# Gate projections moved beside the gated recurrence, experts in 32-row column tiles, and queries padded with zeros

## The chip, the cores and the metric

One core of one Trainium2 chip runs the whole program. The metric is the device time of one execution in microseconds (us). TensorE (PE) multiplies, VectorE (DVE) and ScalarE (ACT) work on rows, GpSimd (POOL) issues the scatters, SyncE (SP) issues the loads and stores.

## The reference

Everything is float32. `first_block` adds to x (512 tokens of 1024) the sum of an attention branch and a recurrent branch, each through a gate projected from the same normed rows h:

```python
o_b = rms_norm(o_fwd + o_bwd, hg_norm_w[layer]) * jax.nn.silu(g_b.reshape(B, S, HG_HEADS, HG_DV))
y_b = jnp.einsum('bsc,cd->bsd', o_b.reshape(B, S, HG_WIDTH), w_proj_b[layer].astype(f32))
merged = jax.nn.sigmoid(zgate_a) * y_a + jax.nn.sigmoid(zgate_b) * y_b
h_res = h_res + jnp.einsum('bsd,de->bse', merged, w_out[layer].astype(f32))
```

Then two layers work on x and, in the first of them, on 256 context rows as well. Layer 0 mixes with a dense attention and a convolution, layer 1 with a recurrence and an attention over a neighbourhood (8 heads of 64, 512 queries, local keys and 256 context keys). Each ends with 16 experts that choose their tokens: 64 of x, and in layer 0 also 32 of the context, each through w1, w3 and w2 of 1024x1024:

```python
hid = jax.nn.silu(jnp.einsum('becd,edf->becf', xs, w1)) * jnp.einsum('becd,edf->becf', xs, w3)
ys = jnp.einsum('becf,efd->becd', hid, w2) * gate[..., None].astype(h.dtype)
```

## The kernel before

The program is written by hand, engine by engine, with semaphores. Every float32 matmul is two instructions in the trace, so an "x4" in an order of instructions is "x8" in the trace.

**First block.** `first_block` (L1179) runs the attention (`first_attention`, L619), then the gated recurrence (L1023) and the modulation (L1249) turn by turn: `weave` takes one turn of each generator in rotation, with six PSUM banks for the recurrence and two for the other line. The modulation has 48 turns, each one load of 1 MB (two slots, L1284) and four matmuls (L1308), two columns each, at the four column tiles. The recurrence goes through blocks of heads: a head of the block with large products (L1069, L1081, L1098, L1118), then a loop over chunks (update L1128, read-out L1152, both directions). The tail stands behind it (L1199 to L1241): Square of recurrentT (L1204), sums by ones (L1205), L1207, Sqrt (L1210), one reciprocal of 128x4096 (L1212), two multiplications, the g_b projection with Silu (`dense` at L373, activation L1218), a multiplication (L1221), proj_b (L377), the two other gates with Sigmoid (L1231), L1234 and L1236, 32 transposes, w_out, whose results are added to the rows at L1239. `dense` loads weights 2 MB at a time in a ring; L373 is its form with the weights stationary and the tokens moving, L377 that with the tokens stationary. `core.settle(engine)` lets an engine wait until everything loaded and computed so far is there.

**Experts of layer 0.** `experts` (L1501) has a ring of six slots of 2 MB, each half of the columns of a weight, in rows of 512 columns (L1550). Per expert, 128 matmuls hold a 128x128 tile of weights and move the 96 tokens (L1574), and 16 hold 96 columns of hidden values and move 512 columns of w2 (L1588). Silu is at L1604, the product at L1617, two scatters per expert add to `row_sums` and `context_sums`. Layer 1 has 64 tokens per expert and does it otherwise: `experts_in_tiles` (L1668) holds 64 columns of tokens in each of two column tiles and moves the weights (L1737).

**Neighbourhood.** `neighbourhood` (L2618) gives 32 units (8 heads x 4 tiles of 128 queries) to `attend` (L1953): scores (L1989, keys and queries on 64 rows, two heads in the halves of 128 partitions), transposes (L2041), weights times values (L2069). The dense attention of layer 0 uses the same `attend` with 96 rows.

## Time and profile before

| | us |
|---|---|
| runs timed | 5477.23, 5398.36, 5399.64 |
| their median | 5399.64 |
| profiled execution, its own time | 5478.97 |
| its span | 5477.2 |
| mean granted clock of TensorE | 0.824 of full speed |

| stage | from | to |
|---|---|---|
| recurrence beside modulation | about 796 | 1284 |
| tail of the first block | 1284 | 1619 |
| experts of layer 0 | 2564 | 3290 |
| units of the neighbourhood | about 4547 | 4730 |
| experts of layer 1 | about 4920 | 5477 |

The stages stand one behind the other, so a stage that gets shorter by some us brings its whole gain to the end unless the next one waits for something else. In the rows below "start us, us" are the start and the busy time of a run of like instructions, "xN" is their count, and the bracket at the end gives the idle time before them and what ended it. PEclk is the granted clock: 1.00 is full speed (2.4 GHz), 0.50 the half (1.2 GHz).

### The profile page before, as it was taken

To read this page: it belongs to the slowest core of one execution; us is meant where nothing else is said; L and a number is where in the kernel's file an instruction comes from. 1 tells how busy PE (TensorE), PEld (TensorE's weight loads), DVE (VectorE), ACT (ScalarE), POOL (GpSimd) and SP (SyncE) were. 2 spreads that over 40 slices of the span, in tenths; PEclk is the share of its full clock that TensorE was granted. 3 is DMA by queue.
4 is the path that set the end of the run, shared out by engine and by line. 5 is a ranking of instruction groups with operands and counts; after the bars stand their busy time and mean duration, and the time that the engine had idled before them with its cause. 6 is when DMAs were issued, how large, how long until landed. Compare 5 with 4: busy or idle time off the path is not lost. (4 is left out here: it accounts for less than half of the span.)

```text
span 5477.2 us, 55057 instructions
## 1 busy us (share of the span) xinstructions
PE 4162.9 (76%) x23087; PEld 2861.7 (52%) x23087; DVE 1573.8 (29%) x2699; ACT 649.2 (12%) x1292; POOL 88.1 (2%) x72
## 2 busy tenths in 40 slices
PE   7987879897978245863999996658788579837777
PEld 4674467663434124733777773357677437622222
DVE  2222223234011746522111112354554422230000
ACT  1121010101010012300000000022212101110000
POOL 0000000000000000000000000000000000000000
PEclk9987995767989667986999997877888786668898
DMA  3100223232201000113888861100000010129999
GB/s 115 62 1 31 88 77 108 93 108 98 102 31 52 0 21 1 38 49 130 310 302 300 306 221 62 46 10 2 1 2 2 26 55 12 44 81 383 382 382 340
DMA packets 317051, 612.86 MB, mean 112 GB/s; under 512 B 32380, under 2 KB 68460, under 8 KB 310150
## 3 DMA queue, kind: packets, MB, share of 16 engines
q1 hardware_dynamic: 309574, 588.35, 30.1%
q0 software_dynamic: 7232, 20.98, 1.6%
q8 instruction: 186, 3.05, 0.2%
q14 instruction: 59, 0.48, 0.0%
HBM read 582.94 MB, written 26.36 MB: 111 GB/s over the span
## 5 line engine op out<-in xcount | busy, mean ns | idle before, releaser
L377 PE MATMUL bank<-weights_l,hT_l 128*128 128x512 f32 (+3 forms) x2080 | 714.3, 506 | 56.2 <-DMA weights_l<-in_od_w_in 21.2
L377 PEld LDWEIGHTS bank<-weights_l,hT_l 128*128 128x128 f32 (+1 forms) x2080 | 435.6, 213 | 331.9 <-issue 265.8
L1574 PE MATMUL bank<-expert_tokensT_l,expert_weights_l 128*128 128x96 f32 x4096 | 462.8, 276 | 23.0 <-DMA expert_weights_l<-in_moe_w 23.0
L1574 PEld LDWEIGHTS bank<-expert_tokensT_l,expert_weights_l 128*128 128x128 f32 x4096 | 463.0, 193 | 30.8 <-issue 30.8
L373 PE MATMUL bank<-hT_l,weights_l 128*128 128x512 f32 (+1 forms) x1056 | 384.4, 527 | 46.6 <-DMA weights_l<-in_w_in 23.9
L1737 PE MATMUL bank<-expert_weights_l,expert_tokensT_l 128*64 128x512 f32 x1024 | 258.7, 663 | 113.4 <-DMA expert_weights_l<-in_moe_w 113.4
L373 PEld LDWEIGHTS bank<-hT_l,weights_l 128*128 128x128 f32 x1056 | 203.6, 193 | 226.2 <-issue 184.6
L1737 PEld LDWEIGHTS bank<-expert_weights_l,expert_tokensT_l 128*64 128x64 f32 x1024 | 91.1, 152 | 270.7 <-issue 270.7
L1588 PE MATMUL bank<-expert_weights_l,hidden_l 128*96 128x512 f32 x512 | 223.6, 594 | 10.1 <-DVE hidden_l L1617 10.1
L1737 PE MATMUL bank<-expert_weights_l,hiddenT_l 128*64 128x512 f32 x512 | 129.3, 663 | 45.3 <-DMA expert_weights_l<-in_moe_w 45.3
L377 PE MATMUL bank<-weights_l,mixedT_l 128*128 128x512 f32 x320 | 141.7, 606 | 29.1 <-DMA weights_l<-in_od_w_out 15.0
L1588 PEld LDWEIGHTS bank<-expert_weights_l,hidden_l 128*96 128x96 f32 x512 | 82.2, 163 | 140.4 <-issue 127.7
L1617 DVE TENSOR_TENSOR hidden_l<-silu_l,bank 128x96 f32<-128x96 f32 x128 | 32.6, 255 | 427.6 <-ACT silu_l L1604 427.6
L2041 PE MATMUL bank<-identity,scores_l 128*128 128x128 f32 (+1 forms) x704 | 131.0, 340 | 7.7 <-ACT scores_l L2027 7.7
L2041 PEld LDWEIGHTS bank<-identity,scores_l 128*128 128x128 f32 (+1 forms) x704 | 112.8, 236 | 40.0 <-issue 26.6
L377 PE MATMUL bank<-weights_l,recurrentT_l 128*128 128x512 f32 x256 | 112.4, 601 | 19.4 <-DMA weights_l<-in_w_proj_b 18.4
L1989 PE MATMUL bank<-kT_l,qT_l 64*128 64x256 f32 (+3 forms) x288 | 120.4, 550 | 1.5 <-DVE kT_l L313 1.5
L377 PEld LDWEIGHTS bank<-weights_l,mixedT_l 128*128 128x128 f32 x320 | 62.2, 195 | 107.5 <-issue 107.5
L1896 DVE SCALAR_TENSOR_TENSOR convolved_l<-padded_l,taps_l,convolved_l 128x798 f32<-128x798 f32 x120 | 117.9, 1046 | 1.1
L1128 PEld LDWEIGHTS bank<-values_l,rows 32*128 32x128 f32 x480 | 94.0, 292 | 44.5 <-DVE state_l L1143 33.7
L1800 DVE TENSOR_TENSOR hidden_l<-silu_l,bank 128x512 f32<-128x512 f32 x16 | 11.0, 688 | 362.0 <-PE bank L1737 362.0
L1152 PEld LDWEIGHTS bank<-queries_scaled_l,state_l 128*128 128x128 f32 x480 | 103.8, 320 | 20.5 <-issue 12.0
(435 smaller groups left out, 5095.9 us busy)
## 6 DMA issues: line engine op xcount, KB each, us to landing
expert_weights_l<-in_moe_w SPq DMA_DIRECT2D x192, 2048.0 KB, 18.6
ada_weights_r<-in_ada_w SPq DMA_DIRECT2D x48, 1024.0 KB, 4.9
weights_l<-in_w_in SPq DMA_DIRECT2D x16, 2048.0 KB, 7.9
weights_l<-in_w_in SPq DMA_DIRECT2D x16, 1024.0 KB, 5.1
weights_l<-in_od_w_in SPq DMA_DIRECT2D x7, 1024.0 KB, 5.3
weights_l<-in_ev_w_in SPq DMA_DIRECT2D x3, 2048.0 KB, 10.5
weights_l<-in_od_w_in SPq DMA_DIRECT2D x3, 2048.0 KB, 7.8
weights_l<-in_w_proj_b SPq DMA_DIRECT2D x2, 2048.0 KB, 15.0
```

The lines of the kernel that those rows point to most:

```text
L373: ins = pe.matmul(bank[:n, :m], w_sb[:, k, s:s + n], xT[:, k, t:t + m], start=k == 0, stop=k == kt - 1)
L377: ins = pe.matmul(bank[:rows_of_tile(x), :n], x, w_sb[:, k, :n], start=k == 0, stop=k == kt - 1)
L1128: ins = pe.matmul(kv_bank[i % 2][:, hh * P:hh * P + P], ks[r, c // 4, hh * P:hh * P + P], v[r, c // 4, hc + hh * P:hc + hh * P + P], start ...
L1152: ins = pe.matmul(o_bank[hh][:, c * CH:c * CH + CH], state[:, i % 2, hh * P:hh * P + P], qt[:, hh, c * CH:c * CH + CH], start=False, stop= ...
L1574: ins = pe.matmul(bank[:, m * 256:m * 256 + S], w[:, k, (f % 4) * P:(f % 4) * P + P], xs[:, k, e, 0:S], start=k == 0, stop=k == KT - 1)
L1588: ins = pe.matmul(core.bank[3 + h][:S, :], hid[:, e % 2, f, :], w[:, f, :], start=f == 0, stop=f == KT - 1)
L1617: dve.tensor_tensor(hid[:, e % 2, f, :], act_out[:, g % 3, :], core.bank[g % 3][:, 256:256 + S], ALU.mult).then_inc(hid_done.sem, hid_done ...
L1737: ins = pe.matmul(bank[h * S:h * S + S, :], rows(k), ring[2 * (i % PAIRS) + h][:, k, :], start=k == 0, stop=k == KT - 1)
L1800: dve.tensor_tensor(hid[:, e % 2, :], silu[:, e % 2, :], core.bank[2 + e % 2][:, :], ALU.mult) \
L1896: ins = dve.scalar_tensor_tensor(out=conv[:, c, :], in0=h[:, c, k:k + OUT], scalar=taps[:, c, k:k + 1], in1=conv[:, c, :], op0=ALU.mult, o ...
L1989: ins = pe.matmul(s_bank[n % 2 * 2 + j][:, a:b], q, k, start=True, stop=True)
L2041: ins = pe.matmul(t_bank[m % 2][:b - a, i * P:i * P + P], s[:, n % R, a:b], core.ident[:, :], start=True, stop=True)
```

## The change

`gate_products` is a third generator in `weave`: 48 turns of four matmuls for the g_b, z_b and z_a projections of the first block (weights stationary, tokens moving), with 12 loads of 1 MB into one slot, a copy by ACT and a store of 256 KB to DRAM for every 128 columns. The modulation goes from two slots to one and from two banks to one; the gates have the other. Both branches are kept by columns (proj_a and proj_b transposed). The tail loads the three gates, the attention branch (2 MB each) and the context rows from DRAM, prefetches w_proj_b, and works in halves; `take` multiplies and adds as the banks of proj_b come, and the transposes are gone. `experts_in_strips` stands for `experts`: four column tiles of 32 tokens, weights moving, eight slots of 2 MB with rows of 1024 columns, hidden values turned by `turn`, three scatters per expert into one tensor of sums (the third waits for the second). The buffers lie in X. In the neighbourhood qT gets a plane per head, whose other half is zero, and the keys go in with all 128 rows.

```diff
+        merge_groups(core, I, C, flip, lasting, hT, top, den, u,
+                     ya[:, :, :].rearrange("p t (a n) -> p (t a) n", n=SEQ))
...
-              lambda e, tt, col, n, ps: copy(core, e, ya[:, tt, col:col + n], ps), ready=False)
+              lambda e, ct, t0, n, ps: copy(core, e, ya[:, ct, t0:t0 + n], ps), transposed=True, ready=False)
...
+def gate_products(core, I, hT, w, out, kept):
...
+    landed, copied = core.weights[1], core.emptied_s
...
+    W, DEEP = 2 * P, KT // 2
...
+    chunks = [(j, off, c) for j, off in enumerate((OFF_GB, OFF_ZGB, OFF_ZGA)) for c in range(0, D, W)]
...
+    for j, off, c in chunks:
+        if n:
+            sp.wait_ge(summed.sem, n)
+        weight_load(w[:, :, :], I["w_in"], KT, off + c, W)(sp).then_inc(landed.sem, landed.sixteen())
+        for s in range(0, W, P):
+            for half in range(2):
+                yield True
+                if half == 0:
+                    pe.wait_ge(landed.sem, landed.n)
+                    if n:
+                        pe.wait_ge(copied.sem, at + n)
+                for k in range(half * DEEP, half * DEEP + DEEP):
+                    ins = pe.matmul(bank[:, :], w[:, k, s:s + P], hT[:, k, :], start=k == 0, stop=k == KT - 1)
+            ins.then_inc(summed.sem, summed.one())
+            n += 1
+            act.wait_ge(summed.sem, n)
+            if n > 1:
+                act.wait_ge(stored.sem, 16 * (n - 1))
+            act.copy(out[:, :], bank[:, :]).then_inc(copied.sem, copied.one())
+            sp.wait_ge(copied.sem, at + n)
+            sp.dma_start(kept[j][:, (c + s) // P, :], out[:, :]).then_inc(stored.sem, stored.sixteen())
+    sp.wait_ge(stored.sem, stored.n)
...
-            core.store(spill, ya[:, :, :])
+            core.store(spill, ya[:, :, :].rearrange("p t (a n) -> p (t a) n", n=SEQ))
...
-            with core.beside(6) as other:
+            with core.beside(6) as other, other.scope() as beside:
+                w, rows = beside("gate_weights", [P, KT, 2 * P]), beside("gate_rows", [P, SEQ])
                 weave(gated_recurrence(core, I, C, hT, oT, X[:, NT:NX, :].rearrange("p t (a b) -> p (t a) b", b=HB * P)),
-                      modulation(other, I, C, mod_dram))
-            core.load(X[:, NT:NX, :], I["ctx_2"][0].rearrange("(t p) d -> p t d", p=P))
+                      gate_products(other, I, hT, w, rows, gates), modulation(other, I, C, mod_dram))
...
+                early = prefetch(core, HH, I["w_proj_b"], 0, D)
...
+                    ya, yb, za, zb = (sb3(name, [P, KT, SEQ]) for name in (
+                        "attention_outT", "recurrence_outT", "attention_gateT", "recurrence_gateT"))
...
+                    gates_landed = [Signal(nc, f"gate_landed_{j}") for j in range(3)]
+                    for dst, src, signal in zip((gb, zb, za), gates, gates_landed):
+                        sp.dma_start(dst[:, :, :], src).then_inc(signal.sem, signal.sixteen())
+                    core.load(ya[:, :, :], spill)
+                    core.load(X[:, NT:NX, :], I["ctx_2"][0].rearrange("(t p) d -> p t d", p=P))
+                    half = HH // 2
...
                     core.settle(act)
-                    act.activation(sq[:, :, :], oT[:, :, :], ACT.Square).then_inc(step.sem, step.one())
+                    for a in range(0, HH, half):
+                        act.activation(sq[:, a:a + half, :], oT[:, a:a + half, :], ACT.Square).then_inc(step.sem, step.one())
...
-                    act.activation(gb[:, :, :], gb[:, :, :], ACT.Sqrt).then_inc(step.sem, step.one())
+                    for a in range(0, HH, half):
+                        act.wait_ge(core.emptied_v.sem, core.emptied_v.n - HH + a + half)
+                        act.activation(rstd[:, a:a + half, :], rstd[:, a:a + half, :], ACT.Sqrt) \
+                            .then_inc(rooted.sem, rooted.one())
+                    act.wait_ge(gates_landed[0].sem, 16)
+                    act.activation(gb[:, :, :], gb[:, :, :], ACT.Silu).then_inc(step.sem, step.one())
+                    gated = step.n
...
+                        s = slice(a, a + half)
+                        dve.wait_ge(rooted.sem, i + 1)
+                        linked(dve, core.link_v, dve.reciprocal(rstd[:, s, :], rstd[:, s, :]))
+                        linked(dve, core.link_v, dve.tensor_tensor(oT[:, s, :], oT[:, s, :], rstd[:, s, :], ALU.mult))
+                    dve.wait_ge(step.sem, gated)
+                    dve.wait_ge(landed.sem, landed.n)
+                    for a in range(0, HH, half):
+                        dve.scalar_tensor_tensor(out=oT[:, a:a + half, :], in0=oT[:, a:a + half, :], scalar=w[:, 0:1],
+                                                 in1=gb[:, a:a + half, :], op0=ALU.mult, op1=ALU.mult) \
+                            .then_inc(step.sem, step.one())
+                    for gate, signal in ((zb, gates_landed[1]), (za, gates_landed[2])):
+                        act.wait_ge(signal.sem, 16)
+                        act.activation(gate[:, :, :], gate[:, :, :], ACT.Sigmoid).then_inc(step.sem, step.one())
                     dve.wait_ge(step.sem, step.n)
-                    dve.reciprocal(gb[:, :, :], gb[:, :, :]).then_inc(step.sem, step.one())
-                    dve.wait_ge(step.sem, step.n)
...
-                    dense(core, hT, KT, SEQ, I["w_in"], OFF_GB, D,
-                          lambda e, ct, t0, n, ps: e.activation(gb[:, ct, t0:t0 + n], ps, ACT.Silu),
-                          transposed=True, who=lambda i: "s")
-                    core.settle(dve)
...
-                with core.scope() as sb3:
...
-                    core.load(ya[:, :, :], spill)
-                    dense(core, oT, HH, SEQ, I["w_proj_b"], 0, D,
...
-                        dense(core, hT, KT, SEQ, I["w_in"], off, D,
...
-                        dve.tensor_tensor(y[:, :, :], y[:, :, :], g[:, :, :], ALU.mult).then_inc(step.sem, step.one())
...
-                    transpose_tokens(core, ya, oT, NT, C["ident"])
-                dense(core, oT, KT, SEQ, I["w_out"], 0, D,
...
+                    dve.tensor_tensor(ya[:, :, :], ya[:, :, :], za[:, :, :], ALU.mult).then_inc(step.sem, step.one())
+                    def take(e, ct, t0, n, ps):
+                        linked(e, core.link_v, e.tensor_tensor(yb[:, ct, t0:t0 + n], ps, zb[:, ct, t0:t0 + n], ALU.mult))
+                        return e.tensor_tensor(yb[:, ct, t0:t0 + n], yb[:, ct, t0:t0 + n], ya[:, ct, t0:t0 + n], ALU.add)
+                    dense(core, oT, HH, SEQ, I["w_proj_b"], 0, D, take, transposed=True, who=lambda i: "v", ready=False,
+                          early=early)
+                    dense(core, yb, KT, SEQ, I["w_out"], 0, D,
+                          lambda e, tt, col, n, ps: e.tensor_tensor(X[:, tt, col:col + n], X[:, tt, col:col + n],
+                                                                    ps, ALU.add), who=lambda i: "v", ready=False)
...
-        slot = [sb("ada_weights", [P, DEEP, W]) for _ in range(2)]
-        mod = sb("bias_then_mod", [P, 2, BANK])
...
-            sp.dma_start(slot[i % 2][:, :, :],
...
+            if i:
+                sp.wait_ge(used.sem, i)
+            sp.dma_start(slot[:, :], dram(I["ada_w_2"][block // per], k * P * MOD + block % per * W, [[MOD, P], [1, W]])) \
...
-def experts(core, I, C, X, layer, nx, mod_dram, sel_dram, xs, sums):
+def experts_in_strips(core, I, C, X, layer, mod_dram, sel_dram, xs, sums):
...
+    STRIP = P // 4
...
+    SLOTS = 8
...
-                    eng_ins = sp.dma_start(ring[n % RING][:, :, :], dram(src, h * HALF, [[D, P], [P * D, KT], [1, HALF]]))
...
+                for i, (name, e, half) in enumerate(plan):
+                    if i >= SLOTS:
+                        sp.wait_ge(used.sem, free_at[i - SLOTS])
+                    sp.dma_start(ring[i % SLOTS][:, :, :], dram(I[name][layer, e], half * DEEP * P * D,
+                                                                [[D, P], [P * D, DEEP], [1, D]])) \
...
-                            for k in range(KT):
-                                ins = pe.matmul(bank[:, m * 256:m * 256 + S], w[:, k, (f % 4) * P:(f % 4) * P + P],
-                                                xs[:, k, e, 0:S], start=k == 0, stop=k == KT - 1)
...
-                            ins = pe.matmul(core.bank[3 + h][:S, :], hid[:, e % 2, f, :], w[:, f, :],
-                                            start=f == 0, stop=f == KT - 1)
...
+                def hidden(e, half):
+                    if half == 0 and e:
...
+                    w1, w3 = landed("moe_w1_2", e, half), landed("moe_w3_2", e, half)
+                    for j in range(DEEP):
+                        k = half * DEEP + j
...
+                        def strip(bank, q, w, h, g):
+                            return pe.matmul(bank[q * STRIP:(q + 1) * STRIP, :], xs[:, k, e, g * STRIP:(g + 1) * STRIP],
+                                             w[:, j, h * HALF:(h + 1) * HALF], start=k == 0, stop=k == KT - 1)
+                        for q, (h, g) in enumerate(pairs[:4]):
+                            strip(w1_bank, q, w1, h, g)
+                        for q, (h, g) in enumerate(pairs[:4]):
+                            strip(w3_bank, q, w3, h, g)
+                        for q, (w, (h, g)) in enumerate(((w1, pairs[4]), (w1, pairs[5]), (w3, pairs[4]), (w3, pairs[5]))):
+                            ins = strip(rest_bank, q, w, h, g)
+                    ins.then_inc(used.sem, used.one())
...
+                    for c in range(4):
+                        pe.transpose(turn_bank[:, c * P:c * P + P], hid[:, c * P:c * P + P], C["ident"][:, :])
+                    for c in range(4):
+                        ins = pe.matmul(turn_bank_b[:, c * 2 * STRIP:(c + 1) * 2 * STRIP], hid_b[2 * STRIP:, c * P:c * P + P],
+                                        C["ident"][2 * STRIP:, 2 * STRIP:], start=True, stop=True)
...
+                    for f in range(half * DEEP, half * DEEP + DEEP, 2):
+                        for j in range(2):
+                            for q, (m, g) in enumerate(pairs[:4]):
+                                strip(y_bank, q, f + j, m, g, 0, KT - 1)
+                        for j in range(2):
+                            for q, (m, g) in enumerate(pairs[4:]):
+                                ins = strip(y_bank_b, 2 * j + q, f + j, m, g, j, KT - 2 + j)
...
+                hidden(0, 0)
+                hidden(0, 1)
                 for e in range(NE):
-                    hidden(e)
-                    output(e)
+                    if e + 1 < NE:
+                        hidden(e + 1, 0)
+                    turn(e)
+                    if e + 1 < NE:
+                        hidden(e + 1, 1)
+                    output(e, 0)
...
+                    for i, (j, at) in enumerate(((0, slice(0, P)), (1, slice(0, 2 * STRIP)), (1, slice(2 * STRIP, P)))):
+                        if i == 2:
+                            pool.wait_ge(scattered[1].sem, 16 * (e + 1))
                         pool.indirect_dma_start(
-                            out=sums[1], out_offset=bass.IndirectOffsetOnAxis(ap=idx[0:CAP_C, 1, e:e + 1], axis=0),
-                            in_=ysc[:, e % 2, :], in_offset=None, compute_op=ALU.add) \
...
+                            out=half_rows, out_offset=bass.IndirectOffsetOnAxis(ap=idx[0:at.stop - at.start, j, e:e + 1], axis=0),
+                            in_=ys[j][at, :], in_offset=None, compute_op=ALU.add) \
...
         v = sb("v_and_one", [P, len(V0) + NC, NA_H, NA_D + 1])
-        qT = sb("qT", [P, NA_H // 2, SEQ])
...
+        for c in range(NA_H // 2):
+            dve.memset(qT[NA_D:, 2 * c, :], 0.0).then_inc(step.sem, step.one())
+            dve.memset(qT[:NA_D, 2 * c + 1, :], 0.0).then_inc(step.sem, step.one())
...
-                transpose_tokens(core, x[0], qT, NT, C["ident"])
...
+                def take(e, c, bank):
+                    copy(core, e, qT[:NA_D, 2 * c, :], bank[:NA_D, :])
+                    return copy(core, e, qT[NA_D:, 2 * c + 1, :], bank[NA_D:, :])
+                products(core, NA_H // 2, fill, take, turns)
...
-                r = slice(h % 2 * NA_D, h % 2 * NA_D + NA_D)
...
-                    q = qT[r, h // 2, t * P:t * P + P]
+                    q = qT[:, h, t * P:t * P + P]
...
-                    parts = [((at, LOCAL + CTX), [(at, LOCAL, q, kTt[r, h // 2, a:b]),
...
+                    parts = [((at, LOCAL + CTX), [(at, LOCAL, q, kTt[:, h // 2, a:b]),
```

On TensorE, in the loop of the recurrence, one round before is:

```order
L1128 MATMUL bank<-values_l,rows 128x128 x4
L1152 MATMUL bank<-queries_scaled_l,state_l 128x32 x4
L1128 MATMUL bank<-values_l,rows 128x128 x4
L1152 MATMUL bank<-queries_scaled_l,state_l 128x32 x4
L1308 MATMUL bank<-ada_weights_r,conditionsT_r 2x512 x4
```

and one round after it:

```order
L1131 MATMUL bank<-values_l,rows 128x128 x4
L1155 MATMUL bank<-queries_scaled_l,state_l 128x32 x4
L1131 MATMUL bank<-values_l,rows 128x128 x4
L1155 MATMUL bank<-queries_scaled_l,state_l 128x32 x4
L1209 MATMUL bank<-hT_l,gate_weights_r 128x512 x4
L1357 MATMUL bank<-ada_weights_r,conditionsT_r 2x512 x4
```

Each round has four matmuls more, ahead of the modulation's. On SP, at the start of the tail, before:

```order
L140 DMA rows<-in_ctx 128x2x1024
L140 DMA gain_l<-in_hg_norm_w 128x1
L323 DMA weights_l<-in_w_in 128x8x512 x2
L140 DMA attention_out_l<-rows_spilled 128x4096
L323 DMA weights_l<-in_w_proj_b 128x8x512 x2
```

and after:

```order
L323 DMA weights_l<-in_w_proj_b 128x8x512 x2
L140 DMA gain_l<-in_hg_norm_w 128x1
L1250 DMA gateT_l<-gate 128x4096
L1250 DMA recurrence_gateT_l<-gate 128x4096
L1250 DMA attention_gateT_l<-gate 128x4096
L140 DMA attention_outT_l<-attention_outT 128x4096
L140 DMA rows<-in_ctx 128x2x1024
```

The context rows, for which ACT waits ahead of Square, now stand last of seven. On TensorE, in the experts of layer 0, one expert before:

```order
L1574 MATMUL bank<-expert_tokensT_l,expert_weights_l 128x96 x128
L1588 MATMUL bank<-expert_weights_l,hidden_l 96x512 x16
```

and after:

```order
L1643 MATMUL bank<-expert_weights_l,expert_tokensT_l 32x512 x48
L1659 MATMUL bank<-identity,rows 128x128 x4
L1661 MATMUL bank<-identity,rows 128x64 x4
L1643 MATMUL bank<-expert_weights_l,expert_tokensT_l 32x512 x48
L1678 MATMUL bank<-expert_weights_l,rows 32x512 x48
```

The turn of one expert stands between the halves of the next one's hidden products.

## Rows read from the trace of the kernel before

**Rows 1.** Page, the span in 40 slices: granted clock and GB/s.

```profile
PEclk9987995767989667986999997877888786668898
GB/s 115 62 1 31 88 77 108 93 108 98 102 31 52 0 21 1 38 49 130 310 302 300 306 221 62 46 10 2 1 2 2 26 55 12 44 81 383 382 382 340
```

**Rows 2.** Windows of five stretches: length, then busy us of each engine.

```profile
core 0: us, PE busy (x) PEld busy (x) DVE busy (x) ACT busy (x) POOL busy (x), PEclk, DMA share, GB/s
829.50:887.00 57.50, 57.23 (x245) 43.39 (x248) 16.23 (x52) 0.00 (x0) 0.00 (x0) 0.50 0.33 111
...
4547.00:4730.00 183.00, 181.01 (x618) 143.53 (x619) 56.39 (x184) 33.05 (x62) 0.00 (x0) 0.50 0.04 13
2158.00:2315.00 157.00, 148.38 (x1058) 129.20 (x1056) 95.56 (x261) 52.39 (x119) 0.00 (x0) 1.00 0.02 8
2600.00:3280.00 680.00, 668.92 (x4505) 530.12 (x4503) 78.89 (x189) 31.38 (x125) 41.24 (x30) 1.00 0.82 290
4950.00:5460.00 510.00, 375.73 (x1515) 135.50 (x1511) 21.52 (x30) 17.59 (x30) 21.70 (x14) 0.90 1.05 382
```

**Rows 3.** Timeline of TensorE, two places in the loop of the recurrence.

```profile
838.95 1.89 PE L1308 MATMUL bank<-ada_weights_r,conditionsT_r 128*2 128x512 f32 x8
840.77 2.07 PE L1128 MATMUL bank<-values_l,rows 32*128 32x128 f32 x8
842.77 1.92 PE L1152 MATMUL bank<-queries_scaled_l,state_l 128*128 128x32 f32 x8
...
848.46 1.89 PE L1308 MATMUL bank<-ada_weights_r,conditionsT_r 128*2 128x512 f32 x8
...
1203.72 1.08 PE L1152 MATMUL bank<-queries_scaled_l,state_l 128*128 128x32 f32 x8
1204.73 1.04 PE L1308 MATMUL bank<-ada_weights_r,conditionsT_r 128*2 128x512 f32 x8
1205.70 1.15 PE L1128 MATMUL bank<-values_l,rows 32*128 32x128 f32 x8
```

**Rows 4.** Timeline of the first block's tail.

```profile
1284.47 0.40 SPq L140 DMA_DIRECT2D rows<-in_ctx  x1
...
1292.02 3.62 ACT L1204 ACTIVATE squares_l<-recurrentT_l 128x4096 f32<-128x4096 f32 x1 [105.22 <-DMA gain_l<-in_hg_norm_w]
...
1296.31 9.67 PE L1205 MATMUL bank<-squares_l,ones 128*128 128x512 f32 x16 [16.94 <-ACT squares_l L1204]
...
1311.82 25.75 DVE L1212 RECIPROCAL gateT_l<-gateT_l 128x4096 f32<-128x4096 f32 x1 [5.12 <-ACT gateT_l L1210]
...
1361.67 4.43 DVE L1221 TENSOR_TENSOR recurrentT_l<-recurrentT_l,gateT_l 128x4096 f32<-128x4096 f32 x1 [17.25 <-ACT gateT_l L1218]
...
1379.27 57.21 PE L377 MATMUL bank<-weights_l,recurrentT_l 128*128 128x512 f32 x128 [18.37 <-DMA weights_l<-in_w_proj_b]
...
1618.30 0.69 DVE L1239 TENSOR_TENSOR rows<-rows,bank 128x512 f32<-128x512 f32 x1 [6.18 <-PE bank L377]
```

**Rows 5.** Timeline of both layers' experts.

```profile
2584.97 32.00 PE L1574 MATMUL bank<-expert_tokensT_l,expert_weights_l 128*128 128x96 f32 x256 [23.01 <-DMA expert_weights_l<-in_moe_w]
...
2703.93 13.97 PE L1588 MATMUL bank<-expert_weights_l,hidden_l 128*96 128x512 f32 x32 [0.63 <-DVE hidden_l L1617]
2717.74 28.72 PE L1574 MATMUL bank<-expert_tokensT_l,expert_weights_l 128*128 128x96 f32 x256
...
3289.21 0.37 SPq L140 DMA_DIRECT2D rows<-row_sums  x1
...
4946.36 7.09 PE L1737 MATMUL bank<-expert_weights_l,expert_tokensT_l 128*64 128x512 f32 x32 [1.51 <-DMA expert_weights_l<-in_moe_w]
```

**Rows 6.** Timeline of TensorE, one unit of the neighbourhood, and two rows of layer 0's attention.

```profile
4598.30 2.07 PE L1989 MATMUL bank<-kT_l,qT_l 64*128 64x256 f32 x4
4600.30 2.07 PE L2041 MATMUL bank<-identity,scores_l 128*128 128x128 f32 x8
4602.30 2.16 PE L2069 MATMUL bank<-v_and_one_l,weightsT_l 64*128 64x65 f32 x8
...
2200.64 1.50 PE L2041 MATMUL bank<-identity,scores_l 128*128 128x128 f32 x12
2201.98 1.45 PE L2069 MATMUL bank<-kv_and_one_l,weightsT_l 128*128 128x65 f32 x12
```

353 lines of the change are left out of this document (178 added, 175 removed).

## The prediction

> **What bounds the kernel now.** I read the page's slices first [rows 1]. TensorE's granted clock is between 0.5 and 0.9 in most slices and the DMA is far from full except in the last four, which carry 382 GB/s; so nearly everywhere TensorE is the limit, and the question of each stage is how much it has to do and at which clock. Then the windows of the four stretches that the change touches [rows 2]. In the loop of the recurrence TensorE is busy 57.23 of 57.50 us at clock 0.50. In the neighbourhood it is busy 181.01 of 183 us at 0.50. In the experts of layer 0 it is busy 668.92 of 680 us at 1.00, with the DMA at 290 GB/s. In those of layer 1, with column tiles, it is busy only 375.73 of 510 us and the DMA moves 382 GB/s: there the loads are the limit. Last the timelines of the loop [rows 3], of the tail [rows 4], of the experts [rows 5] and of a unit of the neighbourhood [rows 6].
>
> Durations come from the profiled execution, 5478.97 us (its span 5477.2). It lies 79 us above the median of the runs, 5399.64, and the two other runs lie close together at 5398 to 5400. About 80 us is what one long stage at 0.50 instead of 1.00 costs (the neighbourhood, 183 us, would give back up to 92). The sum is made against 5478.97.
>
> **Experts of layer 0: -140 us.** One period before is 43.2 us, from 2703.93 to the 2747 at which the 13.97 + 28.72 end and the next w2 begins [rows 5]. After it, an expert is 144 matmuls of 32 columns for 128 rows of weights, in groups of four tiles: 24 groups for w1 and w3, 12 for w2, two instructions each per tile. What a group costs in a stream is not in this trace. Bounds: two tiles side by side do 32 instructions of 512 in 7.09 us, 0.44 us per pair [rows 5]; four tiles side by side would do 8 instructions in 0.87 if each tile's two instructions run after each other and the tiles together; the modulation's four tiles alone do 8 in 1.04 with their fill [rows 3]; and if only two tiles could run together it is 4 x 0.44 = 1.76. I take 0.87, the row of the stream. 36 x 0.87 = 31.3, and the turn, 8 small matmuls, about 1.7: 33.0 us. The DMA needs 12.58 MB / 382 GB/s = 32.9 us [rows 2]. Both limits nearly meet, so I take 33.4 a period, 16 x (43.2 - 33.4) = 157 less. Given back: 16 more small loads of gates, numbers and gain at 0.4 to 0.6 us each on SP ahead of the weights, 9 us; at the end the third scatter waits for the second and both must land before the rows are read; the last w2 ends near 3278, the rows are read at 3289.21 [rows 5], 11 us for one landing, and one more is about 8. Together -140. Hidden: Silu and the products by DVE, since a whole expert's period lies between them.
>
> **Tail: -127 us.** Before it lasts from 1284.47 to 1619.0 [rows 4], 334 us: proj_b starts at +94.8, then 57.2 of proj_b, two more gates of the same size, multiplications, transposes and w_out. After it, 2 x 2 MB of w_proj_b, 3 x 2 MB of gates, 2 MB of the branch and 1 MB of context are issued, 13.6 MB, and ACT's settle ahead of Square waits for the last of them: 13.6 / 382 GB/s = 35.7, with the first packet 36.5, where it waited 7.6 before. Queued behind Square are the ones products, Sqrt and the reciprocals, thus all of the chain. Then 3.6 Square, 0.7 to TensorE, 10.4 ones and L1207, 3 Sqrt (with its table), 25.8 for the two half reciprocals, 2 x 2.2 for the multiplications, 5 for the scalar multiplication with Silu(g_b), 4.4 for ya times za: proj_b at +93, so the wait eats what the g_b projection leaves (that was hidden by the reciprocal anyway). Then 57.2 of proj_b, 1.8 for the last take, 56 for w_out: 207. The two gates (2 x 57), the transposes and the additions between leave the path: 334 - 207 = 127. If the loads run at 300 GB/s instead, 10 less.
>
> A rule of the Trainium skill speaks against the first two terms: "DMA: Bandwidth & Descriptors", section Bandwidth, has the HBM side binding at about 358 GB/s per core. By that figure a period would be 35.1 us and the sum about 29 us less. This trace moves 382 GB/s over 510 us [rows 2], and the measurement decides.
>
> **Recurrence beside modulation and gates: +92 us.** The 48 turns of the gates are the work that left the tail. Each is 8 instructions of 128x512. At full clock that is 3.45 us (0.43 x 8, from 57.21 / 128 = 0.447 [rows 4]), at half clock 6.9. About 28 of them stand in full rounds of the loop. A round before is 848.46 - 838.95 = 9.5 us at clock 0.50 [rows 3], and 5.2 us by the rows at full clock (1.97 from 1203.72 to 1205.70, twice the 2.07 of an update and a read-out, 1.0). With the gates it is 8.6 at full clock and 16.4 at half. Why is the loop at 0.50? Its matmuls are on 32 rows or move 32 columns, and where such work fills TensorE the trace grants 0.50 [rows 2, 3]; in the tail and the experts, with 128x512 or 128x96 on full rows, it grants 1.00. With gates both kinds stand in each round, and no row of before has such a mix. Neither end is excluded: the bounds of a round are 8.6 and 16.4. I take 11.2, one third of the way from full clock, as each round then has dense work of the kind that the rows have at 1.00. 32 rounds x 1.7 = 54. Four heads of blocks take three turns each, beside products where TensorE idles some us (+5 each, 20), and the last four turns with nothing to fill, 14. Loads of the one slot: 1 MB lands in some 5 us after the last matmul that used it, inside a round of 11; ends of blocks cost 4. Together 92. The ends: -0.9 x 32 + 39 = +10 (the same other terms at full clock throughout), and 6.9 x 32 + 83 = +304 (the 16 other turns at half clock, 5.2 each).
>
> **Neighbourhood: -70 us.** A unit before is 2.07 + 2.07 + 2.16 = 6.1 us of TensorE, by the window 183 / 32 = 5.7 each, at 0.50 [rows 2, 6]. The scores are then on 128 rows, the rest is unchanged. The same `attend` on 96 rows ran 157 us at 1.00 [rows 2], where eight transposes cost 1.0 (1.50 for 12) and eight products with values 0.97 [rows 6]. So the zeros add no time to an instruction (512 columns move as before) and a unit at full clock is 3.1: 32 x 2.7 = 86 less. Back come 8 us until the clock rises and 6 for eight memsets and eight copies in place of four on DVE and ACT. -72, taken as -70. From the other side: no rise, +6.
>
> **Sum.** -140 - 127 + 92 - 70 = -245: 5479 - 245 = **5234 us**, 3.1% under the median. If the two other runs of before already had the neighbourhood at full clock, that is why they lie at 5399; the changed kernel would then be steadier.
>
> **Rivals.**
> - The recurrence runs at full clock with the gates in it: +10 instead of +92, 5234 - 82 = 5152. For: the tail's dense work has 1.00. Against: 32 of a round's 48 instructions stay small. 0.10.
> - The clock of the neighbourhood stays at 0.50: -70 becomes +6, 5309. For: only a third of a unit's matmuls is changed. Against: layer 0's attention has the same two other thirds. 0.08.
> - A group of four tiles exposes its fill each time, as in the lone group of the modulation: 36 x 1.04 + 1.7 = 39.1 a period, 16 x 5.7 = +91: 5325. 0.08. By the Trainium skill, "TensorE: Matmul & The Clock Gate", Part 3 (packing), three column tiles run 2.38 times as fast as one after another, not three times; the estimate from that is 1.09 us per group and about 5354 us. No run here shows it yet.
> - Slower than before: the loop stays at 0.50 with the gates. Each round then takes 9.5 + 6.9 = 16.4 us and the stage +304 instead of +92: 5234 + 212 = 5446, 0.9% over the median. Its place is the loop's rounds, and it decides from about 14.9 us per round: 32 x 3.7 = 118 more than forecast, and with the other turns' 45 the sum reaches the median. For: all of the loop's first 57 us are at 0.50, at 99% busy. Against: dense products stand in every round. 0.08.
> - Four tiles run only two at a time: 36 x 1.76 + 1.7 = 65 us per expert, 16 x 31.6 = +506: 5740. Against: the modulation's group of 1.04 for 8. 0.04.
>
> **How the numbers follow.** The forecast has 0.62, with its own range 5180 to 5290 from the round (10 to 13 us: 5195 to 5290) and the loads. With the rivals at 0.10, 0.08 and 0.08 on both sides the range is 5150 to 5330; it leaves out the two slower rivals and half of the exposed fill. A measurement of this kernel tells about 2% from no change: faster than 5291.6 has 0.75 (forecast 0.60, full clock 0.10, part of the second rival), within 2% 0.20, over 5507.6 0.05.
>
> **What would show it.** Right: periods of 33 to 34 us in the experts with the DMA near 380 GB/s; the loop's clock between 0.6 and 0.9 and rounds of 10 to 13 us; a wait of some 36 us ahead of Square, ended by the context rows, and a tail of about 207 us; the neighbourhood at 1.00 in about 105 us. Wrong: a group of four at over 1 us in the experts' stream; rounds at 15 us or more; a neighbourhood window at 0.50; or TensorE waiting at the gates for their slot, which would add up to 5 us in each of 12 loads, 60 us.

## The result, and the profile after

The changed kernel takes 5210.96 us (median of 4 runs, 5206.3 to 5212.48) where the kernel before, in 4 runs, takes 5422.14 (5398.36 to 5477.23): ratio 0.9595, 95% interval 0.9512 to 0.9678. Forecast were 5234 us, in a range of 5150 to 5330. The kernel before scatters by 80 us from run to run, the changed one by 6; the experiments on the neighbourhood bear on this. The two profiled executions are compared stage by stage; 5477.2 and 5204.5 us are their spans. Each border but the last, the end of the program, is an instruction that both kernels have (the first product of the recurrence, the first load of the tail, the loads of modulation, selection, sums and spilled rows).

| stage | before | after | change | forecast |
|---|---|---|---|---|
| recurrence beside other lines | 488.3 | 586.2 | +98 | +92 |
| tail of the first block | 334.7 | 205.4 | -129 | -127 |
| layer 0 up to its experts | 901.1 | 898.4 | -3 | 0 |
| experts of layer 0 | 769.0 | 618.9 | -150 | -140 |
| recurrence of layer 1 | 1073.4 | 1073.7 | 0 | 0 |
| neighbourhood and its projections | 458.9 | 370.2 | -89 | -70 |
| experts of layer 1 | 655.7 | 655.3 | 0 | 0 |
| sum | | | -273 | -245 |

The page's slices after, beside [rows 1]: the three slices that lie wholly in the first experts now carry 395 to 396 GB/s, and the slice with most of the neighbourhood's units (4293 to 4423 us) is at 0.9 or more.

```profile
PEclk9988798898788857896699988777888879868998
GB/s 106 64 17 33 77 73 108 145 74 134 196 32 36 19 3 19 1 41 50 232 396 395 395 276 42 57 1 2 2 2 2 3 83 13 63 150 383 381 381 337
```

The windows that answer to [rows 2], in the order loop of the recurrence, experts of layer 0, units of the neighbourhood, experts of layer 1:

```profile
core 0: us, PE busy (x) PEld busy (x) DVE busy (x) ACT busy (x) POOL busy (x), PEclk, DMA share, GB/s
829.50:887.00 57.50, 53.18 (x245) 32.27 (x245) 14.10 (x45) 1.76 (x3) 0.00 (x0) 0.81 0.43 142
...
2600.00:3080.00 480.00, 478.51 (x4400) 157.44 (x4396) 41.82 (x60) 30.70 (x60) 62.77 (x43) 1.00 1.02 389
4370.00:4463.00 93.00, 91.65 (x630) 80.93 (x631) 56.18 (x183) 31.34 (x65) 0.00 (x0) 1.00 0.09 27
4680.00:5190.00 510.00, 371.64 (x1508) 134.20 (x1504) 22.27 (x31) 18.19 (x31) 22.14 (x15) 0.90 1.05 380
```

The loop went from 0.50 to 0.81, the neighbourhood from 0.50 to 1.00. In the experts TensorE is busy in all but 1.5 of 480 us while the DMA share is 1.02: both are full. Layer 1 is as it was.

The timeline of TensorE in one round of the loop, the counterpart of [rows 3]:

```profile
1000.92 1.15 PE L1131 MATMUL bank<-values_l,rows 32*128 32x128 f32 x8
1002.00 1.08 PE L1155 MATMUL bank<-queries_scaled_l,state_l 128*128 128x32 f32 x8
1003.01 1.15 PE L1131 MATMUL bank<-values_l,rows 32*128 32x128 f32 x8
1004.10 1.08 PE L1155 MATMUL bank<-queries_scaled_l,state_l 128*128 128x32 f32 x8
1005.01 5.38 PE L1209 MATMUL bank<-hT_l,gate_weights_r 128*128 128x512 f32 x8
1010.32 1.04 PE L1357 MATMUL bank<-ada_weights_r,conditionsT_r 128*2 128x512 f32 x8
...
1018.57 5.54 PE L1209 MATMUL bank<-hT_l,gate_weights_r 128*128 128x512 f32 x8 [3.03 <-DMA gate_weights_r<-in_w_in]
```

The small products run at full clock now (1.15 and 1.08 where [rows 3] had 2.07 and 1.92), and the gates pay for it: their eight instructions take 5.38 us, not the 3.60 of a turn at full clock (so at 1237.8 us), since the clock drops inside them: over the four small products from 1000 to 1005 us it is 1.00, over the gates' turn from 1005 to 1010.3 it is 0.68. A round is 10.4 us, only 0.9 more than before without any gates. The last row is the exception that recurs: a turn that needs a new load can find it not landed.

The tail, against [rows 4]. The chain runs as forecast, step by step:

```profile
1382.54 1.03 SPq L323 DMA_DIRECT2D weights_l<-in_w_proj_b  x2
...
1389.91 0.51 SPq L140 DMA_DIRECT2D rows<-in_ctx  x1
...
1418.20 3.71 ACT L1257 ACTIVATE squares_l<-recurrentT_l 128x2048 f32<-128x2048 f32 x2 [42.40 <-DMA rows<-in_ctx]
...
1433.40 12.95 DVE L1273 RECIPROCAL recurrence_outT_l<-recurrence_outT_l 128x2048 f32<-128x2048 f32 x1
...
1468.68 4.42 DVE L1285 TENSOR_TENSOR attention_outT_l<-attention_outT_l,attention_gateT_l 128x4096 f32<-128x4096 f32 x1
...
1473.16 7.38 PE L373 MATMUL bank<-recurrentT_l,weights_l 128*128 128x512 f32 x13 [40.52 <-DVE attention_outT_l L1285]
```

Square starts 35.7 us after the first load (36.5 forecast), ended by the context rows, and proj_b 90.6 after it (93 forecast).

An expert of layer 0, against [rows 5]:

```profile
2706.87 10.48 PE L1678 MATMUL bank<-expert_weights_l,rows 128*32 128x512 f32 x96
2717.17 10.48 PE L1643 MATMUL bank<-expert_weights_l,expert_tokensT_l 128*32 128x512 f32 x96
2727.58 0.66 PE L1659 MATMUL bank<-identity,rows 128*128 128x128 f32 x4
2728.17 1.10 PE L1661 MATMUL bank<-identity,rows 64*128 64x64 f32 x8
2729.20 10.51 PE L1643 MATMUL bank<-expert_weights_l,expert_tokensT_l 128*32 128x512 f32 x96
2739.53 10.48 PE L1678 MATMUL bank<-expert_weights_l,rows 128*32 128x512 f32 x96
```

One period is 2739.53 - 2706.87 = 32.7 us where it was 43.2, and 96 instructions, twelve groups of four tiles, take 10.30 to the next run: 0.86 us per group.

### The profile page after: what moved, and what is told of

It reads as the page before. It is cut to its first block and busy times, and to the rows that moved or that the text cites. A ratio compares the mean times of both kernels' runs of the same rounds, so it can differ in the third digit from the quotient of the medians.

```text
span 5204.5 us, 55236 instructions
## 1 busy us (share of the span) xinstructions
PE 3831.4 (74%) x23247; PEld 2336.5 (45%) x23247; DVE 1537.9 (30%) x2590; ACT 656.2 (13%) x1227; POOL 114.6 (2%) x88
## 5 line engine op out<-in xcount | busy, mean ns | idle before, releaser
L377 PE MATMUL bank<-weights_l,hT_l 128*128 128x512 f32 (+2 forms) x1824 | 605.1, 494 | 60.9 <-DMA weights_l<-in_od_w_in 26.4
L377 PEld LDWEIGHTS bank<-weights_l,hT_l 128*128 128x128 f32 x1824 | 387.5, 216 | 274.8 <-issue 208.6
L1643 PE MATMUL bank<-expert_weights_l,expert_tokensT_l 128*32 128x512 f32 x3072 | 340.6, 600 | 33.0 <-DMA expert_weights_l<-in_moe_w 28.8
L373 PE MATMUL bank<-hT_l,weights_l 128*128 128x512 f32 (+1 forms) x928 | 329.0, 518 | 46.7 <-DMA weights_l<-in_w_in 24.0
L1209 PE MATMUL bank<-hT_l,gate_weights_r 128*128 128x512 f32 x384 | 226.3, 744 | 21.3 <-DMA gate_weights_r<-in_w_in 21.3
L1643 PEld LDWEIGHTS bank<-expert_weights_l,expert_tokensT_l 128*32 128x32 f32 x3072 | 99.9, 111 | 258.0 <-issue 252.0
L1678 PE MATMUL bank<-expert_weights_l,rows 128*32 128x512 f32 x1536 | 167.8, 592 | 0.9 <-ACT rows L1718 0.9
L1209 PEld LDWEIGHTS bank<-hT_l,gate_weights_r 128*128 128x128 f32 x384 | 89.3, 244 | 127.3 <-issue 111.6
L1728 DVE TENSOR_TENSOR rows<-rows,bank 128x512 f32<-128x512 f32 x16 | 11.0, 688 | 376.6 <-ACT rows L1710 376.6
L1146 DVE SCALAR_TENSOR_TENSOR state_l<-state_l,exp_cumulative_l,bank 128x128 f32<-128x128 f32 x224 | 63.0, 343 | 183.1 <-PE bank L1155 182.2
L2369 DVE TENSOR_TENSOR rows<-rows,bank 128x512 f32<-128x512 f32 x96 | 66.0, 688 | 147.8 <-PE bank L2360 142.7
## 6 DMA issues: line engine op xcount, KB each, us to landing
weights_l<-in_ev_w_in SPq DMA_DIRECT2D x3, 2048.0 KB, 10.4
```

What stands on the lines that cost most here:

```text
L373: ins = pe.matmul(bank[:n, :m], w_sb[:, k, s:s + n], xT[:, k, t:t + m], start=k == 0, stop=k == kt - 1)
L377: ins = pe.matmul(bank[:rows_of_tile(x), :n], x, w_sb[:, k, :n], start=k == 0, stop=k == kt - 1)
L1146: ins = dve.scalar_tensor_tensor(out=new[:, s], in0=old[:, s], scalar=cum[:, hh, c * CH + edge:c * CH + edge + 1], in1=kv_bank[i % 2][:, s ...
L1209: ins = pe.matmul(bank[:, :], w[:, k, s:s + P], hT[:, k, :], start=k == 0, stop=k == KT - 1)
L1643: return pe.matmul(bank[q * STRIP:(q + 1) * STRIP, :], xs[:, k, e, g * STRIP:(g + 1) * STRIP], w[:, j, h * HALF:(h + 1) * HALF], start=k = ...
L1678: return pe.matmul(bank[q * STRIP:(q + 1) * STRIP, :], rows, w2[:, f % DEEP, m * HALF:(m + 1) * HALF], start=f == first, stop=f == last)
```

## The experiments

All start from the changed kernel and name what differs. Stage lengths are from one profiled execution of each, between the borders of the table above; a stage that nothing touches repeats within 4 us in nearly all of them, the two recurrences within 7 but for one execution named below.

**The old experts again.** `experts` and the two tensors of sums of the kernel before.

```diff
-            experts_in_strips(core, I, C, X, layer, mod_dram, sel_dram, xs, sums)
+            experts(core, I, C, X, layer, nx, mod_dram, sel_dram, xs, sums)
```

> The changed kernel with the experts of layer 0 as they were before (96 tokens moving, weights stationary). Theory: in the trace of the changed kernel this stage is 618.9 us long where it was 769.0, and the stages stand one behind the other, so the whole 150 us comes back: 5211 + 150 = about 5360 us, the stage again at about 769 us. Rival: part of the shorter stage belongs to what comes ahead of it or behind it (the one tensor of sums, the buffers in X), then it is 5300 us or less.

Measured: 5353.41 us (median of 4 runs), 142 more; the stage is 767.0 us long, 148 more, and every other stage is within 2 us. The gain belongs to the stage.

**Row length and TensorE's share in the experts.** Two kernels: each 2 MB load as two of 1 MB in rows of 2 KB, and seven of the 36 groups left out.

```diff
-                    sp.dma_start(ring[i % SLOTS][:, :, :], dram(I[name][layer, e], half * DEEP * P * D,
-                                                                [[D, P], [P * D, DEEP], [1, D]])) \
+                    for m in range(2):
+                        sp.dma_start(ring[i % SLOTS][:, :, m * HALF:(m + 1) * HALF],
+                                     dram(I[name][layer, e], half * DEEP * P * D + m * HALF,
+                                          [[D, P], [P * D, DEEP], [1, HALF]])) \
```

> The changed kernel, but each 2 MB load of expert weights in layer 0 is made of two of 1 MB, in rows of 512 columns (2 KB) as the kernel before had and as layer 1 has, which moves 382 GB/s there. Theory: TensorE sets the period (31.5 to 31.8 us, at 395 GB/s) and the loads have next to nothing to spare; at 382 GB/s an expert's 12.58 MB take 32.9 us, so the stage gets longer by 16 x 1.2 = about 19 us (638). Rival: the length of the rows doesn't matter, layer 1's rate has another cause, and the stage stays at 619 us.

> The changed kernel, but of the third group of four tiles in each step of the hidden products only the first step's is computed; the other seven, 7 of 36 groups per expert, are left out (6.1 us of TensorE per expert). Theory: TensorE and the loads meet at the same period, so nearly nothing is won: the loads then bind, at 395 to 400 GB/s, and the period stays within 0.5 us of now (stage 612 to 619 us). Rival: the loads have room up to 425 GB/s and TensorE alone binds; the period falls to 29.6 us and the stage by 32 us or more.

Measured, one execution each: with short rows 5232.11 us and a stage of 644.7, 26 longer; with groups left out 5206.48 and 614.3, 4.6 shorter. The same window of the two, short rows first:

```profile
2600.00:3080.00 480.00, 459.60 (x4168) 166.10 (x4164) 39.04 (x56) 28.66 (x56) 61.71 (x42) 0.99 1.06 376
```

```profile
2600.00:3080.00 480.00, 416.99 (x3544) 147.78 (x3540) 41.81 (x60) 30.70 (x60) 64.16 (x44) 0.94 1.02 392
```

The first moves 376 GB/s where the changed kernel moves 389, at a DMA share of 1.06. Two things differ in it, the length of the rows and the size of a load (1 MB for 2); the experiment with long rows in layer 1, further down, changes the length alone. The second has 62 us less TensorE work in the window (416.99 against 478.51 busy) and its stage is hardly shorter: the loads take over at once, at 392 GB/s. Its period is even 33.2 us (the mean of 14 from 2599.74 to 3064.97), where TensorE's own in the changed kernel is 32.7; the 4.6 us come from the first experts. So TensorE and the loads meet, as the prediction had it. Less work for TensorE alone gives no more than these 5 us; that faster loads alone would give no more either was not run, it follows from the 1.5 us of 480 in which TensorE is not busy. And one part of the gain is a thing that the prediction did not count: with loads of 1 MB in rows of 2 KB the stage is 645 us, and its gain would be 124, not 150.

**Weights ahead of the small loads.** The first two loads of weights go before the 22 small ones.

```diff
+        for i in range(2):
+            weights(nc.sync, i)
         core.load(half_of[:, :], I["half_rows"])
...
-                for i, (name, e, half) in enumerate(plan):
+                for i in range(2, len(plan)):
```

> The changed kernel, but in layer 0 the first two loads of expert weights are issued ahead of the 22 small loads. Theory: the weights stream starts some 13 us earlier, the first product too (it waits for the last of the small loads, not for weights), and the stage goes from 619 to about 608 us: about 5200 us. Rival: the small loads queue behind 4 MB of weights and TensorE, which waits for all of them, starts as late as now: no difference within 4 us in the stage.

Measured: 5207.79 us (median of 4 runs), the stage 618.5, no difference: the rival. Counted from the start of the stage the first product comes 3 us earlier, but the queue has only its first two loads to work on while SP issues the small ones. Most take 0.5 us each; two of them, behind the 4 MB, hold SP for 7.3 and 3.0 us, where none held it in the changed kernel:

```profile
2526.94 0.92 SPq L1597 DMA_DIRECT2D expert_weights_l<-in_moe_w  x2
...
2548.92 0.36 SPq L140 DMA_DIRECT2D rows<-modulation  x1
...
2551.52 9.61 SPq L1597 DMA_DIRECT2D expert_weights_l<-in_moe_w  x5
```

The third load goes out some 10 us later in the stage than the first one of the changed kernel did, with 4 MB, 11 us of transfer at 382 GB/s (an estimate), done by then: the start is shifted, not shortened.

**The gates behind the recurrence instead of beside it.**

```diff
-                      gate_products(other, I, hT, w, rows, gates), modulation(other, I, C, mod_dram))
+                      modulation(other, I, C, mod_dram))
+                weave(gate_products(other, I, hT, w, rows, gates))
```

> The changed kernel, but the gate projections run as a line of their own behind the recurrence and the modulation, not beside them. Theory: beside the recurrence they cost 98 us, since they raise the clock of its small matmuls; behind it they cost their own 48 turns at full clock, 48 x 3.6 = 173, and 11 loads of one slot that nothing hides, 11 x 5 = 55: about 228, so 5211 + 130 = about 5340 us, with rounds of 9.5 us at clock 0.50 in the recurrence as before. Rival: the gates cost in the loop what they cost alone (nothing is hidden, the clock is what it is); then the difference is the loads alone, under 60 us: 5270 us or less.

Measured: 5420.57 us (median of 10; nine lie between 5410.99 and 5427.23, one at 17340 that nothing here explains), 210 more. The stage is 794.8, 209 more; the recurrence is back at rounds of 9.5 us. Theory and rival were both too low. TensorE's timeline of one load of the gates:

```profile
1331.65 9.23 PE L1209 MATMUL bank<-hT_l,gate_weights_r 128*128 128x512 f32 x16 [6.96 <-DMA gate_weights_r<-in_w_in]
1341.65 7.11 PE L1209 MATMUL bank<-hT_l,gate_weights_r 128*128 128x512 f32 x16 [0.77 <-ACT gate_rows_r L1215]
```

Each of 12 loads costs 7 us of waiting, not 5, then 2.1 us because the granted clock is 0.50 after the wait, until 1336 us (9.23 against 7.11 for the same 16 instructions), and 0.8 for the copy: 12 x (7.0 + 9.2 + 0.8 + 7.1) = 289. The rest, some 17 us, stands ahead of the gates: the modulation's last product ends 501 us after the start of the stage, in the kernel before, with two slots, 483. So gates and single slot together cost 98 us beside the recurrence and 307 behind it. Two thirds are hidden, and in the loop the clock is most of how: a turn adds 5.4 us to a round and the round gets 0.9 longer, so the other products of the round give back 4.5. Some 27 turns stand in such rounds, which makes about 120 of the 209 us, an estimate.

**Two slots for the gates' weights.** The same room, loaded a chunk ahead.

```diff
-        weight_load(w[:, :, :], I["w_in"], KT, off + c, W)(sp).then_inc(landed.sem, landed.sixteen())
...
+        weight_load(w[:, :, i % 2 * P:i % 2 * P + P], I["w_in"], KT, off + c, P)(sp).then_inc(landed.sem, landed.sixteen())
...
+        if n + 2 < len(chunks):
+            load(n + 2)
```

> The changed kernel, but the weights of the gates come in two slots of 128 columns in place of one of 256 (the same room), each loaded a chunk ahead. Theory: some 10 rounds of 13.3 to 14.4 us among rounds of 10.4 are the one slot's load that the next turn waits for, 3 to 3.5 us each: without them 5211 - 30 = about 5180 us. Rival: the shorter rows (512 bytes) land so much later, or the modulation's single slot waits in their place, that nothing is won: 5205 to 5220 us.

Measured: 5195.03 us (4 runs, 5185.98 to 5204.48), 16 less; the stage is 573.3, 13 less. Theory right, size wrong: the expectation had put all rounds of 13 to 14 us down to the load. The page gives what TensorE waited for; the changed kernel first, the two slots second:

```profile
L1209 PE MATMUL bank<-hT_l,gate_weights_r 128*128 128x512 f32 x384 | 226.3, 744 | 21.3 <-DMA gate_weights_r<-in_w_in 21.3
```

```profile
L1215 PE MATMUL bank<-hT_l,gate_weights_r 128*128 128x512 f32 x384 | 223.2, 735 | 0.0
```

21.3 us of waiting in all, now none. The 48 turns stay at 223.2 us, where 48 at full clock are 48 x 3.60 = 173: the clock costs the gates some 50 us, more than their loads did, and some long rounds stay.

**The tail's loads later.**

```diff
-                    core.load(ya[:, :, :], spill)
-                    core.load(X[:, NT:NX, :], I["ctx_2"][0].rearrange("(t p) d -> p t d", p=P))
...
+                    core.load(ya[:, :, :], spill)
+                    core.load(X[:, NT:NX, :], I["ctx_2"][0].rearrange("(t p) d -> p t d", p=P))
```

(The two lines move behind `products` with the ones; the prefetch of w_proj_b, not shown, moves behind the load of the gain.)

> The changed kernel, but in the tail the gain is loaded ahead of w_proj_b, and the loads of the attention branch and of the context rows stand behind the products with ones, so that Square waits for the gain alone. Theory: the 36 us that ACT waits from the first load to Square (1382.5 to 1418.2) are on the path and nothing else is late; Square starts some 5 us into the tail, the three gates land by 28 us and are needed only after the first reciprocals; the tail goes from 205 to about 175 us, 5211 - 30 = about 5180. Rival: the branch and the context rows, issued later, take the place of the wait (the multiplication by the gate waits for them), and the tail stays above 195 us.

Measured: 5178.68 us (5176.9 to 5181.66), 32 less; the tail is 174.7, 31 less:

```profile
1382.15 0.36 SPq L140 DMA_DIRECT2D gain_l<-in_hg_norm_w  x1
...
1399.82 0.38 SPq L140 DMA_DIRECT2D rows<-in_ctx  x1
```

```profile
1384.51 3.71 ACT L1255 ACTIVATE squares_l<-recurrentT_l 128x2048 f32<-128x2048 f32 x2 [9.23 <-DMA gain_l<-in_hg_norm_w]
...
1402.43 3.62 ACT L1268 ACTIVATE gateT_l<-gateT_l 128x4096 f32<-128x4096 f32 x1
```

Square starts 2.4 us after the first load in place of 35.7, and nothing else is late: Silu of the gate, whose 2 MB stand behind 4 MB of w_proj_b, starts as soon as Sqrt lets it.

**The neighbourhood's scores on 64 rows.** Planes, memsets and copies stay; only the operands change.

```diff
+                    r = slice(h % 2 * NA_D, h % 2 * NA_D + NA_D)
-                    q = qT[:, h, t * P:t * P + P]
+                    q = qT[r, h, t * P:t * P + P]
```

> The changed kernel, but the scores of the neighbourhood read only the 64 rows of their head, of queries and of keys; the planes among zeros, the memsets and the copies stay. Theory: the rows that a score matmul fills set the granted clock of the whole stretch; it is 0.50 again, the units take 183 to 189 us in place of 105, and the time is 5211 + 80 = about 5290 us. Rival: the stretch of before was at 0.50 by chance in the profiled execution (its other runs were up to 79 us shorter), and the time stays within 15 us of 5211.

Measured: 5268.73 us (median of 4: 5237.91, 5239.92, 5297.54, 5305.88), 58 more, and in two heaps. The profiled execution is of the longer kind, with a stage of 464.9 us and both halves of the units at the low clock:

```profile
4365.00:4455.00 90.00, 87.33 (x299) 69.46 (x300) 29.41 (x94) 16.89 (x31) 0.00 (x0) 0.52 0.06 18
4455.00:4545.00 90.00, 90.00 (x304) 70.44 (x304) 27.51 (x91) 15.64 (x31) 0.00 (x0) 0.50 0.03 9
```

The same kernel once more, to see where the heaps differ:

> The same kernel as scores_on_64_rows once more, for a second trace: of its four executions two took 5238 and 5240 us and two 5298 and 5306. Theory: the difference lies in the units of the neighbourhood alone, part of which runs at full clock in the shorter ones (32 units in about 125 us instead of 183); every other stage is as in the first trace within 4 us. Rival: it lies in another stage, then the units take 183 us in both. If this execution falls on the long side, it shows only that the long kind repeats.

Measured, one execution: 5256.35 us, between the heaps, with a stage of 409.9 us, 55 shorter than in the first trace. The windows of its units:

```profile
4379.00:4400.00 21.00, 18.30 (x63) 14.31 (x64) 8.34 (x25) 4.69 (x7) 0.00 (x0) 0.59 0.06 20
4400.00:4440.00 40.00, 40.00 (x137) 31.81 (x137) 11.25 (x39) 7.49 (x15) 0.00 (x0) 0.50 0.04 10
4440.00:4480.00 40.00, 40.00 (x239) 32.12 (x238) 21.71 (x70) 11.56 (x24) 0.00 (x0) 0.95 0.10 31
4480.00:4511.00 31.00, 30.90 (x199) 25.16 (x198) 17.42 (x58) 9.08 (x20) 0.00 (x0) 1.00 0.05 13
```

Same program, same work: the clock is 0.50 for the first 60 us, then rises in the middle of the units and stays. The rest of the two executions agrees within 3 us but for the recurrence of layer 1, 17 longer in the second, so "every other stage is as in the first trace within 4 us" does not hold; without these 17 us the time would be that of the shorter heap. Then the same with only the last four heads on 64 rows:

```diff
+                    r = slice(h % 2 * NA_D, h % 2 * NA_D + NA_D) if h >= NA_H // 2 else slice(0, P)
```

> The changed kernel, but of the neighbourhood's eight heads only the first four read 128 rows in their scores; the last four read 64. Theory: the rows decide; the first 16 units run at granted clock 1.00 in about 52 us, the last 16 fall to 0.50 some time after they begin and take 52 to 94 us. Rival: once the clock is up it stays up, and all 32 units take 105 us as in the changed kernel.

Measured, one execution: 5218.32 us, a stage of 376.0 against 370.2. The rival. The last 16 units, on 64 rows, from 4420 on:

```profile
4422.00:4450.00 28.00, 28.00 (x177) 22.54 (x176) 15.55 (x53) 8.96 (x20) 0.00 (x0) 1.00 0.11 29
4450.00:4474.00 24.00, 23.90 (x156) 19.57 (x155) 13.09 (x44) 7.15 (x15) 0.00 (x0) 1.00 0.00 1
```

So scores on 64 rows do not by themselves bring the clock down. Where it does come down is at the first unit. The end of the projections and the start of the units, the kernel before first and the changed one second:

```profile
4535.00:4547.50 12.50, 9.91 (x45) 6.00 (x43) 5.62 (x11) 2.06 (x5) 0.00 (x0) 1.00 0.00 0
4547.60:4560.00 12.40, 11.01 (x36) 8.51 (x37) 2.93 (x11) 3.25 (x5) 0.00 (x0) 0.50 0.00 0
```

```profile
4350.00:4370.00 20.00, 17.17 (x62) 9.20 (x60) 5.78 (x12) 2.91 (x6) 0.00 (x0) 1.00 0.00 0
```

The projections leave TensorE at 1.00 in every trace. In the first unit TensorE waits twice, 0.8 and 2.2 us, whatever the rows. With 64 rows in it the clock is at 0.50 within 4 us of the unit's start in all three traces (before and the two of this kernel), for 61 us in one and for all units in the others. With 128 rows in the first units it stays at 1.00 through all units in all eleven traces, this one with its later 64 rows included. The zeros don't raise the clock; in the first units they keep it from falling. The later units have no such waits, and more work at 1.00 behind them; which of the two lets 64 rows keep the clock there, no run separates.

**Long rows in layer 1.** The finding on row length, used where the change had not been; a load stays at 2 MB, only its rows get longer.

```diff
-                        sp.dma_start(ring[r][:, :, :], dram(I[names[what]][layer, e], h * HALF,
-                                                            [[D, P], [P * D, KT], [1, HALF]])) \
+                        sp.dma_start(ring[r][:, :, :], dram(I[names[what]][layer, e], h * (KT // 2) * P * D,
+                                                            [[D, P], [P * D, KT // 2], [1, D]])) \
```

> The changed kernel, but the experts of layer 1 load their weights as those of layer 0 now do, in halves of the rows (4 KB pieces) in place of halves of the columns (2 KB). Theory: layer 1 waits for its loads at 382 GB/s, and short rows cost layer 0 26 us; with long rows the loads run at 396 and a period goes from 33.6 to about 32 us: 5211 - 25 = about 5186. Rival: layer 1's rate is set by something else (the scatters, the order of waits), and it stays within 6 us of 5211.

Measured: 5183.19 us (4 runs, 5182.5 to 5191.55), 28 less; the stage is 627.2 where it was 655.3, the period 31.9 us where it was 33.65. The window of layer 1's experts reads 403 GB/s, where the same window of the changed kernel reads 382:

```profile
4680.00:5150.00 470.00, 351.89 (x1466) 129.96 (x1464) 20.81 (x29) 17.58 (x30) 21.73 (x14) 0.92 1.03 403
```

**All three together** (two slots, later loads, long rows in layer 1).

> The changed kernel with two slots for the gates' weights, the later loads of the tail and the long rows in layer 1 together. The stages stand one behind the other, so the gains add: 13 + 31 + 25 = 69, about 5142 us. Rival: if the stages lean on each other, less than two thirds of it, over 5165 us.

Measured: 5134.38 us (median of 6, 5122.06 to 5145.54), 77 under the changed kernel; against the runs of the kernel before taken beside it the ratio is 0.9397, interval 0.9352 to 0.9443. The stages are 572.3, 171.9 and 625.9 us, as each alone, and the gains add up.

## Why the prediction was right

The sum was built from stages that stand one behind the other, and each came out on its own: +98 for +92, -129 for -127, -150 for -140, -89 for -70.

- **Experts.** The group of four tiles at 0.87 us, taken from the pairs' stream and not from the lone group of 1.04, measured 0.86; the period 32.7 us for 33.4. From the first product to the last the experts take 160 us less (157 forecast); the start gave back 5.5 us where 9 were put, the end 4.7 where it was 8. The rivals of an exposed fill and of two tiles at a time are out. The Trainium skill's 2.38 for three tiles ("TensorE: Matmul & The Clock Gate", Part 3) gave an estimate of 1.09 us per group; the trace doesn't agree. The Trainium skill's 358 GB/s per core ("DMA: Bandwidth & Descriptors", Bandwidth) is passed by 395 GB/s. What the prediction took for granted was 382 GB/s for any row length; the rows had changed to 4 KB, and with loads of 1 MB in rows of 2 KB the stage was 26 us longer.
- **Tail.** Every step as written, within 3 us. That the wait for the context rows was on the path is shown by the kernel without it, 32 us shorter.
- **Recurrence.** That +98 lies so near +92 is luck: the terms were off on both sides. The round, "I take 11.2", was 10.4, so 32 rounds add 29 us and not 54. All the rest, the turns at the heads of the blocks, the last four and the loads, was put at 38 us and is 69. The loads of the one slot were put inside a round, with 4 us for the ends of blocks; TensorE waited 21.3 us for them, and two slots took 13 off. A turn at full clock was put at 3.45, with 0.43 for the 0.447 of the row; it is 3.60. The thought that dense work in each round lifts the clock was right, but it is the small products that get it (1.15 us for 2.07), and the gates run slower than at full clock. With the gates behind, the price was 307 us and the time 5421.
- **Neighbourhood.** "A unit at full clock is 3.1" is right: the 32 units take 96.2 us, 3.0 each, where they took 188.7. The term of -70 was under-sized against the profiled execution: the units give 92.5 us where 86 were put, and the "8 us until the clock rises" were none, since it never fell; the memsets and copies cost 5.9 for the 6 put, and what follows the units is 2 shorter: -89. The cause as the prediction put it, that 128 rows have 1.00 and 64 rows 0.50, holds for the first units only: in the later ones 64 rows run at 1.00 as well. What the prediction suspected of the scatter, that the shorter runs of before had this stage at full clock, fits the two traces of one kernel that are 55 us apart in this stage; of before itself no second trace was taken, so for that kernel it is not shown.
- **Against the median.** The gain is 273 us between the two profiled executions and 187 us against the shortest run of before, which lies at 5398. The forecast started from 5479, at the upper end of the three runs it knew. That was the usual time: beside the experiments the kernel before ran 31 times more, and of all 35 runs 23 lie at 5463 to 5487, 7 at 5433 to 5449 and 5 at 5398 to 5404, with a median of 5476. Against that median the changed kernel is 265 us shorter, against the 5422 of the table's four runs 211.

## What to carry to other kernels

Put dense products into a loop of small ones where both need doing: here 48 turns cost 98 us inside the loop and 307 us after it, in large part by the clock that the small ones then get. When loads set the pace, look at the length of their rows first: 4 KB for 2 KB was worth 28 us in layer 1, and in layer 0, where the loads were twice as large too, 26. And before a wait that gathers all loads, ask which of them the next instruction reads: two large loads moved behind it and a small one ahead took 31 us off.
